# A two-layer kernel's second layer: first pass written out by hand in units of two heads, and an opening in halves

## The reference, cut to what matters

```
def second_block(x, ...):
    proj = rms_norm_2(x, ln_mix_g) @ w_in            # 2560 columns: q, k, v, gate v, gate u
    a_out = gmlp_spatial_gating(u, v, ...)           # gelu(u) * (w_s @ norm(gelu(v)) + b_s), blocks of 128
    b_out = banded_chunk_attention(q, k, v, ...)     # 8 heads of 64, chunks of 64 with 8 left chunks
    x = x + concatenate([a_out, b_out]) @ w_out
    return x + peer_ffn(rms_norm_2(x, ln_ffn_g), w_query, sub_keys, peer_u, peer_v)

def peer_ffn(x, ...):                                # per token and head: top 16 x top 16 of 128 keys
    sc = q . sub_keys;  s_top, i_top = top_k(sc, 16) # the 16 best pairs name 16 of 16384 experts
    h = gelu(sum(expert_u[eidx] * x));  y = sum(softmax(best) * h * expert_v[eidx])
```

## Time and profile before

| | us |
|---|---|
| median of 3 runs (3307.12 to 3312.48) | 3311.65 |
| the profiled execution | 3310.64 |
| its span, first to last instruction | 3308.4 |
| PE busy | 2668.5 (81%) |
| DVE / ACT / POOL busy | 1589.2 / 1039.2 / 579.2 |
| layer two, from the last addition of layer one | about 1717 to 3308 |
| of that, before the first gather | 1717 to 1904 |

### The profile page before, as it was taken

How to read it: one execution, slowest core, us unless ns; L and a number is a source line. 1 busy time by engine, 2 the same in 40 slices (tenths; PEclk the granted TensorE clock), 3 DMA queues, 4 the chain that set the end, 5 groups by cost and what they waited for, 6 DMA issues and landing times.

```text
span 3308.4 us, 43725 instructions
## 1 busy us (share of the span) xinstructions
PE 2668.5 (81%) x17232; PEld 1358.6 (41%) x17232; DVE 1589.2 (48%) x3421; ACT 1039.2 (31%) x2445; POOL 579.2 (18%) x536
## 2 busy tenths in 40 slices
PE   8999987886999999999979878787778655555556
PEld 6677774582333333333338744342324211111111
DVE  4656655752101110010026366667675577777664
ACT  2534443420000000000014154577454344344333
POOL 0000000000000000000000034433444344444442
PEclk9999997997999999999989889898979877787777
DMA  3311302338999999999964299999999999999998
GB/s 149 107 45 67 131 10 108 145 124 355 427 427 427 427 427 426 427 427 427 427 279 160 98 373 420 417 404 360 408 420 420 374 420 420 420 420 420 420 420 344
DMA packets 128732, 1068.83 MB, mean 323 GB/s; under 512 B 14352, under 2 KB 16272, under 8 KB 27664
## 3 DMA queue, kind: packets, MB, share of 16 engines
q0 software_dynamic: 75456, 543.20, 40.0%
q1 hardware_dynamic: 53072, 522.86, 38.4%
HBM read 1052.63 MB, written 13.37 MB: 322 GB/s over the span
## 4 chain that ended last, share of the span: by engine, by line
PE 54%; DMA 27%; DVE 10%; ACT 6%; issue 2%; POOL 1%; ACTq 0%; SPq 0%; DVEq 0%; POOLq 0%
PE ps L92 52%; DMA gb<-in_peer_uv,eidx 25%; DVE gb L146 2%; PE ps L97 2%; ACT L168 1%; DMA ga<-in_ed 1%; ACT dots L168 1%; ACT diag L168 1%; POOL gb L86 1%; DVE expert_act L115 1%; ACT prob L168 1%; ACT jk L168 0%; DVE w_lo L115 0%; DVE prob L146 0%; DVE x L115 0%
## 5 line engine op out<-in xcount | busy, mean ns | idle before, releaser
L92 PE MATMUL ps<-gb,diag 64*64 64x512 f32 x4096 | 658.1, 757 | 435.8 <-ACT diag L168 424.4
L146 DVE CUSTOM_DVE_ANT_0 gb<-gb,xn 128x1024 f32<-128x1024 f32 x512 | 626.4, 1224 | 366.2 <-DMA gb<-in_peer_uv,eidx 365.9
L86 POOL DMA_INDIRECT gb<-in_peer_uv,eidx x512 | 565.3, 1104 | 985.9 <-PE ps L92 721.4
L92 PEld LDWEIGHTS ps<-gb,diag 64*64 64x64 f32 x4096 | 149.8, 155 | 873.3 <-ACT diag L168 761.1
L92 PE MATMUL ps<-gw,xt 128*64 128x512 f32 x1008 | 296.0, 602 | 1.7 <-ACT xt L168 1.7
L92 PE MATMUL ps<-ga,xt 128*64 128x512 f32 x1024 | 279.4, 598 | 0.0
L115 DVE TENSOR_TENSOR expert_act<-expert_act,ps 128x512 f32<-128x512 f32 x32 | 22.0, 687 | 527.6 <-PE ps L92 527.1
L168 ACT ACTIVATE dots<-dots 128x1 f32<-128x1 f32 (+1 forms) x378 | 76.7, 203 | 632.1 <-DVE dots L146 626.8
L115 DVE TENSOR_TENSOR x<-x,ps 128x512 f32<-128x512 f32 (+1 forms) x98 | 62.7, 644 | 356.3 <-PE ps L92 355.5
L168 ACT ACTIVATE diag<-cons,dots 128x128 f32<-128x128 f32 x512 | 205.5, 401 | 42.3 <-ACT dots L168 1.5
L168 ACT ACT_TABLE_LOAD x139 | 178.3, 1283 | 9.3 <-PEq L2729 0.7
(11 more groups left out here) (326 smaller groups left out, 3613.3 us busy)
## 6 DMA issues: line engine op xcount, KB each, us to landing
ring<-in_wt SPq DMA_DIRECT2D x77, 1024.0 KB, 6.1
ga<-in_eg SPq DMA_DIRECT2D x33, 2048.0 KB, 28.4
gw<-in_eu SPq DMA_DIRECT2D x32, 2048.0 KB, 33.7
gw<-in_ed SPq DMA_DIRECT2D x32, 2048.0 KB, 32.1
ga<-in_ed SPq DMA_DIRECT2D x32, 2048.0 KB, 33.8
gw<-in_eg SPq DMA_DIRECT2D x31, 2048.0 KB, 25.7
ga<-in_eu SPq DMA_DIRECT2D x31, 2048.0 KB, 31.1
p_scratch<-spill SPq DMA_DIRECT2D x35, 256.0 KB, 2.1
```

Of the source, the lines that this page charges most:

```text
L86: self.e.indirect_dma_start(out, None, table, bass.IndirectOffsetOnAxis(ap=idx, axis=0)).then_inc(s, 16)
L92: i = self.e.matmul(out, l, r, start=st, stop=sp, skip_group_check=True)
L146: self.done(self.e.tensor_tensor_reduce(out=o, in0=a, in1=b, scale=scale, scalar=start, op0=o0, op1=o1, accum_out=acc), name)
```

## The change

1. Opening (`pe_start`, `dv_start`, `ac_start`): X is normed and transposed in two halves of two blocks; the first two tiles' products are ordered so that those that need only the rounded part of the features come first ("coarse"), the others after ("fine").
2. End of layer one: the last eight "put" products get eight banks of their own (`LAST_PUT`), and their additions move into layer two's program.
3. Pass 0 is no generator any more but written out (`pe_first`, `ac_first`, `dv_first`, `sp_first`). One step of attention is two heads of a block, 8 steps for 16 units; ACT makes the rounded part of the tiles from the third on; gelu is done once for all columns and not tile by tile; the two norms share one square root; the `w_s` mask goes from POOL to DVE. The output projection is taken apart by its eight parts k: the parts of attention are multiplied as soon as their heads are ready, block 0's remaining parts first; block 0's norm, features, one query tile for head 0 (as rows, then turned), its scores and choice then run beside block 1's part of the projection. Block 1's X goes through an identity product into PSUM and comes back by ACT.
4. The first choice of experts ends inside `dv_first`; the remaining query tiles come between rows; experts are chosen at first one head ahead, two from row 40; pass 1 begins at row 24 and takes a step each 3.1 rows (before: row 4, 3.6 rows).
5. The seven first buffers have another order and other conditions; two of them hold weight tiles before.

```
-        for c in range(8):
-            pe.wait_ge("ident", ("xn_a", 2), ("xn_a", 3))
-            for i in range(4):
-                pe.tr(PS[c][:, 128 * i:128 * i + 128], XNa[:, i, 128 * c:128 * c + 128], ident, ("tr_h", c) if i == 3 else None)
...
+        for i2 in range(2):
+            for c in range(8):
+                pe.wait_ge("ident", ("xn_a", 2 * i2), ("xn_a", 2 * i2 + 1))
+                for i in (2 * i2, 2 * i2 + 1):
...
+        coarse(0)
+        fine(0, range(4))
+        coarse(1)
+        fine(0, range(4, 8))
+        fine(1, range(8))
+        for n in range(2, 11):
...
+    LAST_PUT = [XBK, DBK, GBK, UBK]
...
+        for t in range(11):
+            if t < 8:
+                hp, j, n = units2(t)[:3]
+                for e in range(2):
+                    ...
+                    pe.mm(ps[:, 0:n], q2[HALF[e], hp, 128 * j:128 * j + 128], k2_[HALF[e], hp, 0:n], name=("s_ps2", 0, t) if e else None)
+                half(*fill[t])
+            for k, j in parts.get(t, ()):
+                wo_part(k, j)
...
+        for n in range(4):
+            for k in range(4):
+                wo_part(k, 0, (n,))
+        for n in (2, 3):
+            for k in range(4):
+                wo_part(k, 1, (n,))
+        feature(0)
+        for k in range(4):
+            wo_part(k, 1, (1,))
+        rows_of_query(0)
...
+        dv.wait_ge(("n_sq", 0), ("n_sq", 1))
+        dv.ts(v, v, 1e-6, ADD)
+        dv.stt(w, v, 1e-6, w, MUL, ADD, name="n_var")
...
+        head = dv_choose(dv, 0, 0)
+        for step in range(STEPS - 2):
+            next(head)
...
-    ROW_BUFFERS = [(t, 0, None) for t in EARLY] + [(THIRD, 0, ("used", 19))]
+    ROW_BUFFERS = [(t, 0, None) for t in EARLY[2:]] + [(THIRD, 0, ("used", 10)), (EARLY[0], 0, ("used", 13)), (EARLY[1], 0, ("used", 14))]
...
-        done, p, owed = 0, 2, []
-        pass_rows = [4 + 18 * k // 5 for k in range(51)]
+        done, p, owed = STEPS, 2, []
+        pass_rows = [24 + 31 * k // 10 for k in range(51)]
...
-            need = min(32 * STEPS, STEPS * (32 + group[-1]) // 16)
+            ahead = 16 + min(8, n) + max(0, min(8, (n - 8) // 4))
+            need = min(32 * STEPS, STEPS * (ahead + group[-1]) // 16) if n > 2 else STEPS
             while done < need:
-                if done % 13 == 0 and p < 8:
+                if done >= STEPS + 2 and done % 18 == 11 and p < 8:
...
-    def po_mix2(po):
-        po.wait_ge("w_s")
-        po.tt(ws, ws, row3(cons[:, C_WM:C_WM + 128], 8), MUL, name="w_s_m")
```

More of the change, by code:

```diff
@@ L1631, in pe_moe @@
                 for n in range(2):
-                    b, use, before = xt.next()
+                    if c < 7 or i == 0:
+                        b, use, before = xt.next()
+                    else:
+                        b, before = LAST_PUT[i][n], [("gated", 7, 1)]
                     pe.wait_ge(("ye", c), ("place", c), *before)
@@ L1789, in sp_pass @@
[L1789 to L1803, removed]
+        elif s < 13:
+            sp.wait_ge(("w2lo", s - NS))
+        elif s < 15:
+            sp.wait_ge(("used", 8))
+        elif s < 17:
+            sp.wait_ge(("used", 27 - s))
+        else:
+            sp.wait_ge(("used", s - 2))
@@ L1804, in sp_pass, with sp_second @@
+    def sp_second(sp):
+        for m in range(6):
+            sp_tile2(sp, TILES + m)
+        sp.wait_ge(("n3", "x", 3))
+        sp.dma(rowb, I["rows"][:, 1024:2048], "row_gain", ("ffn_g", 1))
+        sp_bias(sp, 0)
+        sp_bias(sp, 1)
         for m in range(6, 9):
-            sp_tile2(sp, p, m)
+            sp_tile2(sp, TILES + m)
         for h in range(2, 8):
[L1807 to L1818, removed]
+            sp_bias(sp, h)
+            if h < 5:
+                sp_tile2(sp, TILES + 7 + h)
+        for m in range(12, 22):
+            sp_tile2(sp, TILES + m)
@@ L1973, in features @@
                     yield
-        if p == 0:
-            for c2 in range(4):
-                b, _, _ = turn.next()
-                ac.wait_ge(("g_ps", 0, c2))
-                for c in (2 * c2, 2 * c2 + 1):
-                    ac.act(gH[:, c, :], PS[b][:, 256 * (c % 2):256 * (c % 2) + 256], ACT.Copy, scale=col(K_MIX2 + c), name=("g_hi", c))
-        else:
-            yield from features("g", "g_ps", gT, K_MIX2)
+        yield from features("g", "g_ps", gT, K_MIX2)
         for x in range(2):
@@ L2140, in dv_pass @@
         head_scale(1)
-        split2(6)
         yield
@@ L2282, in peer_order @@
                     p += 1
-                if done % 13 == 6 and owed:
+                if done % 18 == 1 and owed:
                     yield owed.pop(0)
@@ L2504, in dv_peer @@
     def dv_peer(dv):
[L2505 to L2508 removed]
+        few = few_turn()
+        dv_first(dv, few)
         dv.signals("dve_peer")
[L2510 removed]
+        turn, wide, _ = second_turns()
         second = dv_pass(dv, 1, turn, wide)
```

648 lines of the change are left out of this document (534 added, 114 removed).

## The result

The changed kernel takes 3255.28 us (median of 4 runs, 3253.24 to 3258.32) for 3311.59 of the kernel before (3307.12 to 3312.48): a ratio of 0.9833, 95% interval 0.9816 to 0.9850, 56.3 us faster. The forecast was 3258, its range 3238 to 3284.

What follows compares the result with a forecast made beforehand. Computing bounds the kernel up to the first gather, transfers at 420 GB/s after it. Opening -3.3, the stretch to the gather -53.0 (reserve included), early idle -7.4, pass 1 +10: -53.7, median about 3258 us, range 3238 to 3284.

Steps and rivals of the forecast that it cites:

- Opening: Start of layer one: halves bring the second chunk out at about 27.6 us, and layer one moves as a whole, -3.3 us.
- Norms: End of layer one to layer two's first tile: earlier squares, one root and the mask on DVE save 13.5 us.
- Tiles: First tile to first scores: a tile still costs 5.65 us; 1.2 us better than the shift alone.
- Attention and projection: First scores to block 0's X: filler keeps PE busy at 2.4 GHz, 64.4 us for 91.4, -27.0 us.
- X to scores: Block 0's X to the first scores out: one block and half a query tile, 12.3 us for 27.2, -14.9 us.
- rival 5: First choice of experts: held by block 1's late root, first gather +10, 3268 us; chance 0.07.
- Reserve: Ahead of the first gather: 3.6 us put for small waits between three in-order engines.
- Behind the first gather: First gather to end: less early idle, -7.4 us; pass 1 squeezed into 155 rows instead of 180, +10 us.
- 2: Attention: the written order stalls and half of the old units' wait returns, 20 us given back, 3278 us; chance 0.15.
- 4: Rows 24 to 179: row chain plus pass step needs more than the transfer, so slower than before; chance 0.04.
- 1: Pass 1 behind the first gather: squeezed hard, +25 instead of +10, 3273 us; chance 0.16.
- 3: Whole kernel: pass 1 costs nothing and the waits are nil, 3244 us; chance 0.12.

Runs made afterwards that it cites:

- e10: The changed kernel with the w_s mask moved back from DVE to POOL: 3258.4 us, ratio to before 0.9842.
- e5: The changed kernel with five pieces of output projection moved from attention's steps 8 to 10 to behind its last step: 3261.1 us, ratio to before 0.9848.
- e13: The kernel before with only pass 1's steps at the changed kernel's rows (24 + 3.1k for 4 + 3.6k): 3304.0 us, ratio 0.9976.
- e12: The changed kernel with pass 1 at 2.9 rows a step in place of 3.1: 3250.4 us, ratio to before 0.9818.
- e6: The changed kernel with the rounding of all second-layer tiles given back from ACT to DVE: 3260.3 us, ratio to before 0.9846.

## Why the prediction was right, point by point

The time was right to 2.7 us. What set the time ahead of the first gather was right too, while the two terms behind it were each wrong by 17 to 20 us and cancelled: in that part the good sum is luck.

- **Opening, -3.3.** The second chunk is out at 29.17, not at 27.6, and from the third on the lead is 1.4 us (35.19 for 36.59). "Moves as a whole" was wrong: nothing of it is left at 497. That layer one still ended 6.7 us earlier in the trace comes from places without an edit, the largest with a higher granted clock, and not from the working I gave.
- **Norms, -13.5: -10.3.** The first product comes 18.2 us behind `ye`, for 28.4 before. Of the 3.2 us that are missing, 2.3 are some that I had not seen: DVE's cast and subtraction of the second tile (1701.87 to 1705.42) stand ahead of the first addition, which starts 4.77 us behind `ye` and not 2.45 as before (1709.94). The 2.0 us of the mask were right (e10), and no 3.25 us row is left.
- **Tiles, -1.2: -0.9.** A tile takes 5.87 us, not 5.65.
- **Attention and projection, -27.0: -31.8.** The filler was right (e5: without the five pieces 6.8 us come back, clock and all); what the half tiles, the order of the projection and the pairs of heads are worth each was not run. The size: I gave sixteen units 1.03 us each beside the tile; what is left of the 59.56 after tiles, 14.0, 7.0, 3 and 0.7 is 12.3, that is 0.77 a unit. It was not a wait that I had read into the 1.03: PE was busy for all of 1774.89 to 1805.79, at 1.00. What I overlooked is that a step now has two heads, whose products fill half of PE each (64*128 for the scores, 128*64 for the values), and that two such products take the time of one. The scores of two heads (x4, two records for a product) take 0.49 us at 1756.95, as those of one head (x2) did at 1774.89, and the next instruction starts 0.42 and 0.41 us behind them. The products with `v` of two heads took 0.88 us at 1775.48; before, those of one head:
```profile
1793.02 0.86 PE L92 MATMUL ps<-prob_t,v 128*64 128x256 f32 x4
```
By these rows scores and values of sixteen units cost 7 us less in pairs (8 score steps at 0.4 to 0.6 us and 4 value steps at 0.8 us saved). Less of it shows against the 1.03, since the old eight units that it comes from had only two of the eight value steps. No run has the pairs taken apart.
- **X to scores, -14.9: -15.3,** and the choice unchanged (10.57 for 10.30). Block 1's root did not hold it: the root is ready at 1831.9 and DVE comes for it only later (ACT waits 2.22 us for DVE, not the reverse), which rules out rival 5 for this trace.
- **Reserve, +3.6:** not needed. The stretch from `ye` to the first gather shrank by 58.1 where the four terms say 56.6.
- **Behind the first gather, -7.4 + 10: +7.6.** Three sizes are wrong here and cancel in part. Early idle, -7.4: in the first 100 us it fell by 5.0, but a 15 us hole came behind, so that the first 175 us lost 9.5 more than before. Pass 1's squeeze, +10: 17 us did not become 27 but 8 (-9.7); e13 shows that these rows alone are worth 7.5 us, e12 that fewer rows a step go on helping. I had argued that a step's transfer shrinks while its computing stays. What fails in that, the runs do not show; a computation that is spread over fewer rows need not cost more in sum. And 8.1 us of transfer, put at nothing: I took 27 weight tiles behind the first gather for before, where the trace has 24, and wrote that the change takes no bytes away; it brings three tiles and a little more behind the first gather (27 transfers of 1 MB). In the changed program each of the last five tiles of pass 0 waits for the buffer of the tile two before it (`("used", s - 2)`), and those are the query tiles that now stand among the rows. Time for them there was: from 1797 to 1816.5 the DMA engines moved 1 GB/s.
```profile
1797.00:1816.51 19.51, 19.26 (x105) 16.56 (x104) 6.08 (x9) 3.46 (x5) 0.00 (x0) 1.00 0.00 1
```
- **Rivals.** 2 (stalls, low clock) is ruled out by the clock of 1.00 and 4 by the time itself. 1 stands on the squeeze and falls with it (e13). 3 said idle of pass 1 costs nothing; that was nearest, but without the 8.1 us of transfer.
- **The signs.** Clock of 1.00 in attention and no 3.25 us row: as said. Four table loads up to the first gather, I said five; the first gather at 1839.05, I said 1847.6; from there to the end 1412, I said 1407. Missed: the first product comes 9.1 us behind the last addition of blocks 0 and 1 (1709.92 to 1718.98), and not within 8; the first 50 us behind the first gather ran at 390 GB/s, where no window was to be under 400; and pass 1's attention has less shortfall than 17 us, not more.

In the profile the first gather came 8.6 us earlier than forecast (3.4 of it in layer one, 3.6 the reserve), and the rest was 5.1 longer. Ahead of the first gather each term was right to 5 us. Behind it the terms were off by +17 (early idle), -20 (pass 1) and +8 (bytes), and only their sum was near.

## What to carry to other kernels

When work is moved from ahead of a transfer-bound stretch into it, count the transfers that wait for its buffers: they move with it and are paid at full price (here 8.1 us of the 65 by which the first gather came earlier). Fill the waits of a small in-order pipeline with the next stage's products; here this also kept TensorE's granted clock up (1.00 for 0.85 without, in 1789 to 1797). Products of two heads that fill half of PE each, put together, took the time of one. A schedule of background steps among rows is best measured at two paces before its price is argued: here idle that looked like too much work a row fell when the steps stood denser.

## What the runs showed of the hardware

- The granted clock of a stretch whose code is unchanged differs between executions (480 to 510 us: 0.89 and 1.00, with starts 0.4 us apart), worth 3.5 us at one place; ends of layer one scatter over 6 us in eleven executions of the same layer one.
- Two products that fill half of PE each, of two heads, take the time of one: 0.49 us for four records at 1756.95 as for two at 1774.89, and 0.88 for eight at 1775.48 as 0.86 for four at 1793.02.
- A DVE operation on 2 columns takes 2.18 us for 0.16 while POOL multiplies in SBUF (e10).
- An activation starts within 0.02 us of the end of a table load in the changed kernel too (ACT):
```profile
1757.73 1.28 ACT L168 ACT_TABLE_LOAD   x1
1759.03 0.40 ACT L168 ACTIVATE prob<-prob,small 128x128 f32<-128x128 f32 x1
```
- Kernels with identical code behind the first gather differ there by up to 5 us of idle (54.2 in e5 and 59.2 in e6), most of it at 300 to 450 us behind it (403 and 390 GB/s); what decides it is open.
